# Last head of a recurrent mixer: two remainders move to GpSimd, three weight roundings move ahead of table functions

## The reference, cut to what matters

```
z = h @ w_in                      # g = z[:, :D], rec = z[:, D:]
u = depthwise_conv(rec)
r, i = sigmoid(u @ wa + ba), sigmoid(u @ wx + bx)      # per head, per direction
a = exp(-8 r softplus(-lam));  b = sqrt(1 - a*a) * (i * u)
y = scan_forward(a, b) + scan_backward(a, b)
out = (gelu(g) * y) @ w_out
x = x + gate * rms_norm(out)
```

## Time and profile before

| what | us |
|---|---|
| median of 3 runs | 1995.94 (1995.64 to 1998.39) |
| the profiled execution | 1998.64 |
| its span | 1996.9 |
| TensorE busy | 1949.2 (98%) |
| VectorE busy | 1669.1 (84%) |
| GpSimd busy | 1278.9 (64%) |
| ScalarE busy | 992.2 (50%) |

### The profile page before, as it was taken

One profiled execution on the slowest core, in us unless ns is written; L12 is line 12 of the kernel. 1 busy time (PEld: TensorE's weight loads), 2 busy tenths in 40 slices (PEclk: granted clock), 3 DMA queues, 4 the chain that ended last, 5 costly groups with the idle time before them and its releaser, 6 DMA issues. The chain is left out here.

```text
span 1996.9 us, 27938 instructions
## 1 busy us (share of the span) xinstructions
PE 1949.2 (98%) x8774; PEld 1587.8 (80%) x8774; DVE 1669.1 (84%) x1769; ACT 992.2 (50%) x1419; POOL 1278.9 (64%) x856
## 2 busy tenths in 40 slices
PE   7999999999999999999999999999999999999997
PEld 3777777788888888888888788878888888888886
DVE  5588888978789889999988875797889888888888
ACT  4867768556544444444444545573333334333333
POOL 4544234575877788888778983465676655656765
PEclk9999999999999999999999988799999999999998
DMA  8222322540222223222223320211111111111114
GB/s 327 96 95 84 121 83 86 200 169 32 87 88 88 95 94 95 85 83 92 87 95 95 120 112 11 95 53 54 63 53 53 53 53 63 52 53 63 52 53 169
DMA packets 78016, 179.74 MB, mean 90 GB/s; under 512 B 5104, under 2 KB 28944, under 8 KB 77328
## 3 DMA queue, kind: packets, MB, share of 16 engines
q1 hardware_dynamic: 77968, 179.13, 26.6%
HBM read 166.52 MB, written 12.58 MB: 90 GB/s over the span
## 5 line engine op out<-in xcount | busy, mean ns | idle before, releaser
L2936 DVE TENSOR_TENSOR Y<-Y,ps 128x1024 f32<-128x1024 f32 x280 | 324.2, 1212 | 3.1
L2238 POOL TENSOR_TENSOR So_lo<-So_raw,So_hi 128x512 fp32r<-128x512 f32 x120 | 199.1, 1666 | 198.7 <-DVE So_raw L2872 167.6
L1770 ACT ACTIVATE So_hi<-So_raw 128x512 fp32r<-128x512 f32 x180 | 112.8, 627 | 148.7 <-POOL So_raw L2230 76.0
L2009 POOL TENSOR_TENSOR red<-red,E_quad 128x512 f32<-128x512 f32 x77 | 124.9, 1621 | 60.4 <-ACT E_quad L1824 57.5
L1770 ACT ACTIVATE WB_hi<-rawB 128x512 fp32r<-128x512 f32 x120 | 74.9, 631 | 165.7 <-PE ps L1202 111.7
L1962 POOL TENSOR_TENSOR WA_lo<-rawA,WA_hi 128x1024 fp32r<-128x1024 f32 x20 | 57.9, 2893 | 149.2 <-DVE u L2573 108.1
L1770 ACT ACTIVATE WA_hi<-rawA 128x512 fp32r<-128x512 f32 x120 | 73.3, 627 | 121.4 <-PE ps L1222 83.1
L1202 PE MATMUL ps<-T_hi,So_hi 128*128 128x512 f32 x336 | 131.2, 391 | 0.0
L1202 PE MATMUL ps<-T_hi,So_lo 128*128 128x512 f32 x336 | 130.8, 389 | 0.0
L1202 PE MATMUL ps<-T_lo,So_hi 128*128 128x512 f32 x336 | 130.7, 389 | 0.0
L1202 PE MATMUL ps<-H_hi,WA_hi 128*128 128x512 f32 x336 | 130.7, 389 | 0.0
(11 more groups left out here) (441 smaller groups left out, 6328.4 us busy)
## 6 DMA issues: line engine op xcount, KB each, us to landing
rawA<-wA SPq DMA_DIRECT2D x62, 512.0 KB, 3.3
rawB<-wB SPq DMA_DIRECT2D x62, 512.0 KB, 3.3
E_quad<-ada SPq DMA_DIRECT2D x44, 512.0 KB, 3.5
quad<-ada SPq DMA_DIRECT2D x8, 2048.0 KB, 9.4
rawB<-wC SPq DMA_DIRECT2D x22, 512.0 KB, 3.9
rawA<-wC SPq DMA_DIRECT2D x20, 512.0 KB, 3.8
ada_first<-ada SPq DMA_DIRECT2D x8, 1024.0 KB, 15.3
outT<-X SPq DMA_DIRECT2D x16, 512.0 KB, 4.6
```

The source lines that it names most:

```text
L1770: A(dst[:, at:at + HF], op_source(name), ACT.Copy).then_inc(op_hi, 1)
L2009: TT(red[:], red[:], E_quad[:, :, k % 2 * P:k % 2 * P + P], ALU.add).then_inc(red_made, 1)
L2238: TT(lo[:, at:at + HF], op_source(name), hi[:, at:at + HF].bitcast(F32), ALU.subtract)\
L2936: TT(at, at, ps[:, bank:bank + 2, :], ALU.add).then_inc(d_added, 1)
```

## The change

GpSimd gets the remainders of (0, 2) and (0, 3), which VectorE made. On ScalarE, the rounding of A(9) moves from behind the exponentials to ahead of them, that of B(9) from behind the square roots to ahead of them, and that of A(10) from behind the last head to ahead of the GELU. On GpSimd the remainder of A(9) moves ahead of the wait for `iu_last` and of the product `IB*u`. Nothing is added or removed in all.

```diff
-        LO_POOL = [(0, 0), (0, 1), (1, 0), (1, 1), (1, 2)]
-        LO_DVE = [(0, k) for k in range(2, KT)] + [(1, k) for k in range(3, KT)]
+        LO_POOL = [(0, 0), (0, 1), (0, 2), (0, 3), (1, 0), (1, 1), (1, 2)]
+        LO_DVE = [(0, k) for k in range(4, KT)] + [(1, k) for k in range(3, KT)]
...
+                if last:
+                    round_hi("A", NH + 1)
                 for d in range(2):
                     A(RA[d][:], RA[d][:], ACT.Exp, scale=s_exp[:, bass.ds(d * NH + hd, 1)]).then_inc(exp_made, 1)
                 if last:
-                    round_hi("A", NH + 1)
                     for k in range(3):
                         gated_hi(1, k)
+                    round_hi("B", NH + 1)
                 for d in range(2):
                     act.wait_ge(tanh_made, 2 * hd + d + 1)
                     A(TH[d][:], TH[d][:], ACT.Sqrt).then_inc(sqrt_made, 1)
                 if last:
-                    round_hi("B", NH + 1)
+                    round_hi("A", NH + 2)
                 A(Y[:, hd], flat(AB67), ACT.Gelu_apprx_tanh).then_inc(g_made, 1)
...
             head(NH - 1, last=True)
-            round_hi("A", NH + 2)
             for k in range(3, KT - 1):
                 gated_hi(1, k)
...
                 if last:
-                    for k in range(2):
+                    for k in range(4):
                         gated_lo(0, k)
                     lo_of_unit("B", hd + 1)
+                    lo_of_unit("A", hd + 2)
                     pool.wait_ge(iu_last, 1)
...
             head(NH - 1, last=True)
-            for n in (1, 2, 3):
+            lo_of_unit("B", NH + 1)
+            for n in (2, 3):
                 for s in "AB":
                     lo_of_unit(s, NH + n)
...
                 if last:
-                    for k in range(2, KT - 1):
+                    for k in range(4, KT - 1):
                         gated_lo(0, k)
```

## The result

| | before | changed |
|---|---|---|
| median of 22 runs each, us | 1996.29 (1994.26 to 1999.94) | 2000.36 (1996.78 to 2002.87) |
| ratio, 95% interval | | 1.0016 (1.0010 to 1.0022) |
| span of the profiled execution, us | 1996.9 | 2001.1 |

The change makes the kernel slower by 0.16%, 3.2 us with an interval of 2.0 to 4.4. The ratio goes by all runs: the medians lie 4.1 us apart, the means 3.2 (1996.69 and 1999.88). The difference is beyond the noise, and at 0.16% inside the 0.2% that the prediction called no change, though its interval reaches to 0.22%. The traced execution of the changed kernel is the slowest of its 22 (2002.87), 2.5 us above their median; that of the kernel before (1998.64) is 2.4 above its own.

The account below looks back on a forecast made before the run. TensorE, busy 1949.2 of 1996.9 us, bounds the kernel. Removable waits and clock of 6.5 us shrink to a 1.6 us lead, lost at VectorE's late sums: -0.05 to +2.05, middle +1.0, so 1996.9 us; range 1992.0 to 1999.6.

Parts of the forecast that it names:

- the likeliest case: TensorE's lead of 1.6 us is used up at L844; +1.0 us, own range 1995.9 to 1998.0, chance 0.60.
- rival C: At L844 TensorE waits 3.65 us and the clock falls behind it: +3.75, or +6.0 with another GpSimd block; chance 0.08.
- Remainders: In m=0, GpSimd's WB_lo cuts into VectorE's remainders; this part costs 0.6 us where it was to save 1.58.
- rival A: In m=0, VectorE keeps its turn against WB_lo and m=0 ends unbroken: 1992.3 to 1993.9 us; chance 0.22.
- Clock in m=0: m=1 starts at 339.65; a clock drop inside m=1 to m=3 would hide behind ScalarE's queue.
- Lead: At m=5, TensorE starts at 361.95 instead of 363.56, a lead of 1.6 us that stays until L844.
- Sums: VectorE's seven sums of squares before L844 end at 391.6, or at 393.75 if WA_lo(13) gets in between.
- Clock behind L844: After TensorE's wait at L844, no clock fall was counted in the forecast; a slower rival counted 1.7 us.

Follow-up runs that it names:

- e4: Changed kernel with GpSimd's WB_lo(8) made to wait until VectorE's three remainders are done; 1.0012 of the kernel before.
- e7: Changed kernel with GpSimd's WA_lo(13) held until VectorE's seven sums of squares are done; 1.0000 of the kernel before.
- e2: Kernel before with only the new order of the roundings and of GpSimd's WA_lo(9), VectorE keeping its five remainders; 1.0011 of the kernel before.
- e8: Changed kernel with the rounding of A(9) back behind the exponentials on ScalarE; 1.0017 of the kernel before.
- e3: Changed kernel with TensorE's column sums at L844 and their spreading four pieces later in its list; 0.9994 of the kernel before.
- e6: Changed kernel with WB_lo(8) behind VectorE's three remainders and L844 four pieces later; 0.9983, then 0.9994 of the kernel before.
- e9: Changed kernel with WB_lo(8) behind VectorE's three remainders, L844 four pieces later and WA_lo(13) held until the seven sums end; 0.9973, then 0.9976 of the kernel before.
- e1: Kernel before with only remainders (0,2) and (0,3) moved to GpSimd, old order of the roundings; 0.9995 of the kernel before.

## Why the prediction was right, and what in it was off

The range held and "same within 0.2%" was likeliest, but the kernel is measurably slower by 3.2 us where I forecast +1.0, the middle of a band from -0.05 to +2.05. The measured ratio puts the kernel at 1999.1 on the scale of the forecast, inside the range up to 1999.6, but its interval, 1997.9 to 2000.3, reaches past it, and nearly all of it lies above the likeliest case's own range, which ended at 1998.0. The path was right link by link up to the sums of squares. What happened there was not the forecast but the smaller form of rival C: its condition (the seventh sum ends later than 393.9) was met with 394.82, its wait of 3.65 us was measured as 3.64, the clock below 1 behind L844 was its sign, and its +3.75 is nearer to the 3.2 than my +1.0. I gave it 0.08. So the number stayed inside the range in part by luck. The list of chances also set C wholly above 1999.9, though its own lower sum gives 1999.7.

- **Remainders.** I had VectorE's list start at 334.7, (0,5) reach TensorE at 338.15 and (0,6) end at 338.7. Measured: 334.61, 338.12, 338.67. Alternation against WB_lo was the right reading; rival A did not happen by itself. e4, which forces the turn that A supposes, shows that A was priced wrong too: it left out that TensorE then waits 2.48 us for WB_lo(8) and that the wait at L844 stays, and where A had 2.05 to 3.6 us of gain e4 is 2.4 us slower than the kernel before.
- **Clock in m=0.** I put m=1 at 339.65; it started at 340.49, because the clock fell behind the break. I had allowed for a fall inside m=1 to m=3 and said it would hide behind ScalarE's list; no traced run with the new order of the roundings shows one there. One that begins in m=0 does not hide, since ScalarE's rounding of A(9) waits for the end of m=0. This 0.84 us went through all that followed: roots 349.60 for 348.7, m=5 362.78 for 361.95, the last Y*TH 373.83 for 373.0.
- **Lead.** Forecast 1.6 us at m=5, measured 0.8, and 0.5 where TensorE reached L844 (391.23).
- **Sums.** I had two ends, 391.6 without and 393.75 with WA_lo(13) among them, and took the middle. The block came (the arithmetic said so, by a thin margin, and I should have followed it): 394.82, which is 393.75 and the 0.84 from m=0, and 0.2. e7 puts the block at 2.2 us against my 2.1.
- **Clock behind L844.** This is the term that was wrong. I left it out of the sum, since the clock had stayed full behind the wait of 1.58 at 338.20. The wait was 3.64, as rival C had it, and the fall cost 2.5 us. At L844, e2, e4 and e8, with waits of 3.4 to 3.6, show a fall too; e3, e6 and e7, with 0.9 to 1.5, do not.

With the block and both falls in it the sum is 2.05+0.84+0.2+2.5 = 5.6 us, and the traced stretch is 5.75 longer. The measured ratio is less, 2.0 to 4.4 us. Part of that are 1.5 us that the trace gains later, which I cannot explain. For the rest, the traced execution is the slowest of its kernel, and the timed runs need not all have the block or the fall in m=0, which e3 and e7 did not have; no run tests this.

## What to carry to other kernels

A rounding that waits for TensorE, put ahead of work that others need, ties the whole list of its engine to TensorE's next stall. That is a price and not a ban: the fastest kernel here, e9, keeps the new order and takes away what it costs further on. A lead that is won early is worth nothing if TensorE meets, further on, a sum of another engine that started late; ask for such a sum as late in TensorE's list as its readers allow. And where VectorE and GpSimd share work on two SBUF operands, count every GpSimd instruction that becomes ready inside a VectorE run as time of that run.

## What the runs showed of the hardware

- GpSimd and VectorE take turns even within a chain of seven sums: in the changed kernel the three sums that met a GpSimd operation of 128x1024 took 2.71, 2.44 and 2.64 us, and three that met none took 0.69 each. Keeping one of the three out with a single added wait shortened the chain by 2.2 us (12.27 to 10.09).
- The same waits do not always bring the clock down: behind 0.2 and 1.8 us of idle TensorE in m=0 the granted clock from 336 to 345 was 0.81 in the changed kernel and in e1, but 1.00 in e3 and e7, which have the changed kernel's instructions up to there. In the changed kernel it was down from 339 and m=1 started 0.9 us later than in the other three; in e1 it was down from 340, and m=1 started on time. What made the difference is open.
